# A decoder block on eight cores: the head of the first feed-forward stage is loaded, cast and ordered differently

## The reference

```python
x = x + 0.5 * swiglu_ffn(rms_norm(x, g_ffn1), w_ffn1_in, w_ffn1_out)
h = rms_norm(x, g_mix)
# retention, differential attention, memory attention on h @ w_in, gated and merged into y
x = x + y @ w_o
x = x + 0.5 * swiglu_ffn(rms_norm(x, g_ffn2), w_ffn2_in, w_ffn2_out)

def rms_norm(x, g):      # over the 1024 channels of a token
    return x * rsqrt(mean(x * x) + EPS) * g
def swiglu_ffn(h, w_in, w_out):
    gate, up = split(h @ w_in, 2)      # 2816 each
    return (silu(gate) * up) @ w_out
```

## Time and profile before

| | |
|---|---|
| median of 3 runs | 2390.73 us |
| lowest, highest | 2389.24, 2524.57 us |
| profiled execution | 2388.88 us, of which the span of its slowest core (core 2) is 2387.8 us |
| spans of the eight cores | 2382.2 to 2387.8 us |
| PE busy | 2321.8 us, 97% of the span, 13284 matmuls |
| DVE, ACT, POOL busy | 51%, 41%, 6% |
| chain that ended last | PE 90%, ACT 4%, DVE 2%, POOL 1%, DMA 1% |

### The profile page before, as it was taken

One profiled execution on the slowest core, in us unless ns is written; L12 is line 12 of the kernel. 1 busy time (PEld: TensorE's weight loads), 2 busy tenths in 40 slices (PEclk: granted clock), 3 DMA queues, 4 the chain that ended last, 5 costly groups with the idle time before them and its releaser, 6 DMA issues.

```text
span 2387.8 us, 34149 instructions; the slowest of 8 cores (2382.2 to 2387.8 us)
## 1 busy us (share of the span) xinstructions
PE 2321.8 (97%) x13284; PEld 1112.4 (47%) x13284; DVE 1222.9 (51%) x2359; ACT 984.8 (41%) x1679; POOL 149.8 (6%) x173
## 2 busy tenths in 40 slices
PE   6999999999999999999999999999999999999998
PEld 2444444444444444454444465555554444444443
DVE  5577334485565552113444576677754655344334
ACT  3111110357767764144631487788851221111110
POOL 1000000230000000000000111121100000000000
PEclk9999999999999999999999999999999999999999
DMA  8221221353442424342102200201305322321313
GB/s 232 49 50 24 52 38 34 82 135 58 67 79 37 83 43 74 54 73 51 20 16 46 46 12 10 45 13 28 48 10 141 71 45 36 53 36 24 47 18 141
DMA packets 86779, 132.69 MB, mean 56 GB/s; under 512 B 71648, under 2 KB 72032, under 8 KB 75360
## 3 DMA queue, kind: packets, MB, share of 16 engines
q0 software_dynamic: 10512, 75.50, 18.8%
q1 hardware_dynamic: 76112, 55.00, 9.1%
HBM read 172.43 MB, written 16.78 MB: 79 GB/s over the span
## 4 chain that ended last, share of the span: by engine, by line
PE 90%; ACT 4%; DVE 2%; POOL 1%; DMA 1%; issue 1%; SPq 0%; POOLq 0%; DVEq 0%; ACTq 0%
PE pw L605 90%; ACT ET L616 2%; POOL acc L628 1%; ACT nrs L616 1%; DMA stg<-w_ffn_in 1%; DMA memT<-mem 0%; ACT L616 0%; DVE dq L620 0%; DVE dU L639 0%; ACT sqf L616 0%; SPq L647 0%; DVE mqn L620 0%; DVE dn L620 0%; ACT nsq L616 0%; ACT sgt L616 0%
## 5 line engine op out<-in xcount | busy, mean ns | idle before, releaser
L605 PE MATMUL pw<-hT,wbuf 128*128 128x512 bf16 x4864 | 1168.5, 381 | 12.3 <-ACT nrs L616 5.6
L605 PEld LDWEIGHTS pw<-hT,wbuf 128*128 128x128 bf16 x4864 | 471.5, 98 | 551.9 <-issue 29.4
L616 ACT ACTIVATE sgf<-pw 128x512 f32<-128x512 f32 x176 | 104.1, 596 | 702.6 <-PE pw L605 702.5
L605 PE MATMUL pw<-uu,wbuf 128*128 128x512 bf16 x1408 | 334.1, 379 | 0.0
L605 PE MATMUL pw<-wbuf,hT 128*128 128x512 bf16 x1280 | 303.2, 379 | 0.2 <-DVE sgR L628 0.2
L616 ACT ACTIVATE ET<-pw 128x1024 bf16<-128x1024 f32 (+1 forms) x288 | 265.9, 975 | 66.9 <-PE pw L605 64.0
L628 DVE TENSOR_TENSOR uu<-pw,sgf 128x512 bf16<-128x512 f32 x176 | 120.8, 690 | 275.7 <-PE pw L605 275.5
L605 PEld LDWEIGHTS pw<-uu,wbuf 128*128 128x128 bf16 x1408 | 137.7, 98 | 166.1 <-issue 0.2
L605 PEld LDWEIGHTS pw<-wbuf,hT 128*128 128x128 bf16 x1280 | 123.0, 98 | 137.5 <-issue 0.6
L605 PE MATMUL pw<-Vd,ET 128*128 128x129 bf16 x2176 | 173.2, 220 | 8.3 <-DVE dU L639 4.5
L620 DVE SCALAR_TENSOR_TENSOR xT<-pw,xT 128x512 f32<-128x512 f32 x192 | 130.4, 688 | 78.4 <-PE pw L605 74.7
(11 more groups left out here) (120 smaller groups left out, 2153.6 us busy)
## 6 DMA issues: line engine op xcount, KB each, us to landing
wbuf<-w_in POOLq DMA_DIRECT2D x26, 1024.0 KB, 8.3
wbuf<-w_ffn_in POOLq DMA_DIRECT2D x21, 1024.0 KB, 10.3
wbuf<-w_ffn_out POOLq DMA_DIRECT2D x10, 1024.0 KB, 9.6
xs<-xT SPq DMA_DIRECT2D x4, 2048.0 KB, 11.6
xT<-x SPq DMA_DIRECT2D x6, 1024.0 KB, 22.9
wbuf<-w_br_ret POOLq DMA_DIRECT2D x4, 1024.0 KB, 8.0
wbuf<-w_mem_kv POOLq DMA_DIRECT2D x4, 1024.0 KB, 10.5
x2l<-xs SPq DMA_DIRECT2D x2, 2048.0 KB, 14.5
```

The source lines that it names most:

```text
L605: return Op("pe", lambda e: e.matmul(out, lhsT=lhsT, rhs=rhs, start=start, stop=stop, **kw), reads, writes, n / 2400.0 + 0.003, 0.17, sign ...
L616: return Op("act", lambda e: e.activation(out=out, in_=in_, func=func, **kw), reads, writes, c, 0.08, fuse=("accum_out" not in kw), tab=TA ...
```

## The change

Five edits, all in the head of the stage:

- Tile 0 of `x` comes in two transfers of 1 MB and not four of 0.5 MB, `cbf` between the two and `pvec` behind them. The first half of tiles 2 and 3 is now issued only when the tile before has landed.
- The eight casts of the first block move from POOL to ScalarE, behind the first tile's Exp.
- The first three weight transfers on POOL wait for the first half of tile 1, the second half of tile 2 and the first half of tile 3.
- The order of the products becomes: block 0 with tiles 0 and 1, block 1 with tiles 0 and 1, then blocks 0 and 1 with tile 2, then with tile 3. Block 0 with tiles 2 and 3 is worked bank by bank, no output products are woven into the first four of these, and the evacuation of tile 0 is held back until the Exp of tile 1 has been emitted.
- A matrix of ones is written into `uu19`, and products of it with itself, whose results nobody reads, go into a free bank: 9 ahead of the first tile's squares, 12 between its fourth and fifth, 9 behind its eighth (`warm`).

The diff, cut to its core:

```diff
+        def warm(n):
+            for _ in range(n):
+                yield Op("pe", lambda e: e.matmul(bk(6), lhsT=uu[19][:, 0:128], rhs=uu[19][:, :], start=True, stop=True),
+                         [uub[19]], [bkb[6]], 0.22, 0.17)
...
+                if done == ("f1", "h", 0):
+                    yield Op("dve", lambda e: e.memset(uu[19][:, :], 1.0), [], [uub[19]], 0.2)
+                    yield from warm(9)
...
+                    if done == ("f1", "h", 0) and k in (3, 7):
+                        yield from warm(12 if k == 3 else 9)
...
+                if key[0:4] == ("f1", "u", 0, 0):
+                    yield flag(("f1", "h", 1, 0))
...
-            for b in range(11):
+            order = [(b, t) for b in range(11) for t in range(NT)]
+            if tag == "f1":
+                order[0:8] = [(0, 0), (0, 1), (1, 0), (1, 1), (0, 2), (1, 2), (0, 3), (1, 3)]
+            for n_, (b, t) in enumerate(order):
+                outs = 2 if tag == "f2" or n_ >= 4 else 0
...
-                parts = 4 if t == 0 else 2
+                for i in range(2):
+                    sl = slice(i * 2048, i * 2048 + 2048)
+                    dep = [x1b(t - 1, 7)] if t >= 2 and i == 0 else []
...
         def w_cast():
+            yield flag(("f1", "h", 0, 0))
...
-                yield Op("pool", lambda e, dst=dst, src=src: e.tensor_copy(out=dst, in_=src), [stgb[k]], [w0b[k]], 0.6)
+                yield act(dst, src, AF.Copy, [stgb[k]], [w0b[k]], TT)
...
-            yield flag(("f1", "x0"))
-            for dep in (x1b(3, 0), x1b(3, 0), x1b(3, 7)):
-                yield W.load([dep])
+            for t, k in ((1, 0), (2, 7), (3, 0)):
+                yield flag(("f1", "x", t))
+                yield W.load([x1b(t, k)])
```

More of the change, by code:

```diff
@@ L810, in ffn @@
                 wbk = w0b if (tag, b) == ("f1", 0) else [wb] * KC
[L811 to L833, removed]
+                us, keys = held.setdefault(((b + 1) // 2, t), ([], []))
+                if b == 0 and (tag == "f2" or t < 2):
+                    bks = []
                     for j in range(2):
@@ L837, in ffn @@
                         keys.append((tag, "u", b, t, j))
-                        bks = []
                         for half in range(2):
[L840 to L853, removed]
+                            yield f_all.free
+                            bks.append(f_all.get())
+                    for k in range(KC):
+                        yield flag((tag, "h", t, k))
+                        if tag == "f1":
+                            yield flag(("w0", k))
+                        for i in range(4):
+                            c = k * 512 + (i % 2) * 256 + (i // 2) * 128
+                            yield mm(bk(bks[i]), wt[:, c:c + 128], hs(t, k), k == 0, k == KC - 1, [wbk[k], hTb[t][k]],
+                                     [bkb[bks[i]]], TT)
@@ new lines, in ffn @@
+                    for j in range(2):
+                        sch.spawn(evac(bks[2 * j], bks[2 * j + 1], us[j], keys[j]), 0)
+                    pend.append(outp(0, t, us, keys))
+                    if t == NT - 1:
+                        W.give((tag, "a", b))
+                    continue
+                for j in range(2):
+                    yield uu_s.free
+                    us.append(uu_s.get())
+                    keys.append((tag, "u", b, t, j))
+                    bks = []
+                    for half in range(2):
+                        yield f_in.free
+                        p = f_in.get()
+                        bks.append(p)
+                        for k in range(KC):
+                            yield flag((tag, "h", t, k))
+                            c = k * 512 + half * 256 + j * 128
+                            yield mm(bk(p), wt[:, c:c + 128], hs(t, k), k == 0, k == KC - 1, [wbk[k], hTb[t][k]],
+                                     [bkb[p]], TT)
+                        if half == 0:
+                            yield from steps(outs)
+                    sch.spawn(evac(bks[0], bks[1], us[-1], keys[-1]), 0)
+                    yield from steps(outs)
@@ L854, in ffn @@
+                if b % 2 == 0:
+                    pend.append(outp(b // 2, t, us, keys))
+                if t == NT - 1:
+                    W.give((tag, "a", b))
             yield from steps(99)
@@ L874, in load_consts @@
             for t in range(NT):
-                parts = 4 if t == 0 else 2
-                n = KC // parts
-                for i in range(parts):
-                    if t == 0 and i == 1:
+                for i in range(2):
+                    sl = slice(i * 2048, i * 2048 + 2048)
+                    dep = [x1b(t - 1, 7)] if t >= 2 and i == 0 else []
+                    yield spdma(xT[:, t * 4096 + i * 2048:t * 4096 + (i + 1) * 2048], x_d[t][:, sl], dep,
+                                [x1b(t, k) for k in range(i * 4, i * 4 + 4)], 1 << 20)
+                    if t == 0 and i == 0:
                         yield spdma(cbf[:, :], cbf_d[:, :], [], [b_cbf], 200000)
[L880 to L883, removed]
+                if t == 0:
+                    yield spdma(pvec[:, :], pvec_d[:, :], [], [b_const], 32768)
                 sch.spawn(norm(lambda k, t=t: x1(t, k), lambda k, t=t: x1b(t, k), t, PV_GFFN1, ("f1", "h", t)), 3)
@@ L889, in load_consts @@
                     sch.spawn(w_cast(), 2)
-            flags.add(("f1", "x0"))
+                flags.add(("f1", "x", t))
             yield spdma(keep[:, :], keep_d[:, :], [], [b_keep], 98304)
```

## The result

The changed kernel takes 2375.95 us as a median of 5 runs, against 2390.55 of the kernel before on the same chip. The ratio is 0.994, 95% interval 0.9922 to 0.9957: some 14.5 us less. I had forecast 2383.0 with a range from 2377.5 to 2388.0. The sign and the place were right.

A forecast was written before the change was run, and what follows sets the result against it. TensorE was taken as full behind the head, so only the head's gaps could be won. Gains of 0.95 and 5.9 sum to 6.9 us: 2388.9 to 2382.0; the median stands 1.8 higher, so forecast 2383.0, range 2377.5 to 2388.0.

The forecast's parts named there:

- step 2: Tile 1 in the head: lands at 26.5 us, main run starts at 32.3 instead of 33.25, gain 0.95 us.
- step 3: From tile 1's main run to the first output product: 3.3 us lost in place of 9.2, gain 5.9 us.
- All engines run the same order afterwards: Behind the head: a change of the head can win only what the head loses.
- Step 1: Tile 0 in the head: first product at 19.4 us against 17.21, covered because tile 1 cannot start before its second half lands.
- my slow case: Tile 0: the twelve products of ones run at 0.43 us until 15.4 us, costing 2.2 us at its first product.
- The clock dip: Tile 1's main run: after a quiet stretch 3.0 us run at half pace, losing 1.6 us.
- The stall of 1.2 us: Block 1 to tile 2: tile 2's eighth `hT` ready after 9.8 us, TensorE needs it after 8.6.
- The block that holds back tile 1: Rival: early weight block delays tile 1's landing to 28.4 or 31.4 us, gain 5.0 or 2.0; chance 0.17.
- Ones that never lift the clock: Rival: tile 0 begins at 0.43 us a product, tile 1's run starts at 33.6 to 34, 2383.6 us; chance 0.12.
- It goes better: Rival: tile 1 unhindered, no dip on tile 1, no stall; gain 11.5 us, 2377.4; chance 0.12.
- Tile 2 late: Rival: tile 2 lands at 47.5 and 50.6 us, 7.8 lost against 6.9 gained, 2389.8; chance 0.07, shared with block late.
- marks for "right": Head: tile 0's first product 17 to 20 us, tile 1's run 31 to 33.5, no DMA waits, first output near 59.

The follow-up runs named there:

- second profiles: The kernel before and the changed kernel, both unchanged, each profiled again; 2389.85 us (ratio 0.9997) and 2376.76 us (0.9942).
- run 31: Not a follow-up run: in "From Ln to the run 31.20 - 27.79", tile 1's main run of products in the changed kernel, starting at 31.20 us.
- late: Changed kernel with the first three weight transfers tied to the landing of tile 3 again, as before the change; 2391.19 us, ratio 1.0005.
- nochain: Changed kernel with all of x issued at once, tiles 2 and 3 no longer waiting for the tile before to land; 2387.05 us, ratio 0.9987.
- nohold: Changed kernel without the wait that holds back tile 0's evacuation until tile 1's Exp; 2378.34 us, ratio 0.9949.
- nowarm: Changed kernel without the thirty products of ones; 2380.46 us, ratio 0.9958.
- no_first9: Changed kernel without the first nine products of ones; 2376.22 us, ratio 0.994.

## Why the prediction was wrong, step by step

The gain at the last product was 13.8 us, and my sum had 6.9. Of the some 7 us missing, 2.2 lie in step 2, 1.5 in step 3, and 3.3 behind the head, which I had at nothing. Without the 2.3 us gained near 930 us the time would have been some 2378.3, inside the range.

**What bounds the kernel: right in the main, wrong in one clause, and here the mechanism failed.** "All engines run the same order afterwards" is true, and I took it to mean that nothing moves behind the head. The same order does not give the same time when something outside it, the loading of the program, moves against it. The cost was the 2.3 us gained near 930 us (1.9 between the second profiles), and it was not a term mis-sized but one that I put at nothing without a row to show it.

**Step 1, tile 0: right.** Most of its working came out within 1.3 us: the eighth sum ended at 16.1 (forecast 17.2), the first product of tile 0 came at 18.57 (19.4). `hT` began 1.7 us earlier than forecast (17.57 against 19.3), for it follows the Exp at once. The twelve ones took 4.85 us on this core (5.1) and ran at half pace until 14.09. On the others the pace rose anywhere from 9.2 to 14.5 us, so my slow case was that of the slowest core and not the common one. A cast took 4.25/8 = 0.53 us (0.54), a piece of `hT` 0.67 (0.67). The first half of tile 0 landed at 6.7 and not 8.0; as I said, none of this was on the path.

**Step 2, tile 1: mis-sized, 0.95 forecast, 3.1 measured.** From Ln to the run 31.20 - 27.79 = 3.4 us, exactly the chain I had added up. Three terms were off. The landing: I took 26.5, half shared with the block. It was 24.8 as a mean of the eight cores (24.5 over the six of the ledger), and `late`, without the early block, gives 24.8 too. The block is issued 2 us before tile 1 has landed, and delayed nothing. From the landing to Ln I took 2.4 us, and it took 3.0 over these six; before it had taken 4.2 over all eight, so this stretch too became shorter, which I had not worked out. Together they are 1.4 of the miss (32.3 forecast, 30.94 measured). The rest, 0.8, is the row I measured from: 33.25 is one core's value, and the mean of six was 34.05 (33.58 in the second profile).

**Step 3, what follows: right in kind, too cautious.** Lost from 31.20 to 56.59: 25.39 less 110 products at 0.2157, 1.7 us, where I had 3.3. The clock dip came as forecast: the loads run at half pace from 31.46 to 34.56, 3.1 us (3.0), which costs 1.5 (1.6); this is the slowest core, and on three of the six there was no dip. The stall of 1.2 us before tile 2's eighth `hT` did not come. I had let the chain of ScalarE start when a whole group of block 1 was done; Silu needs the gate's eight products alone, so it starts 8 x 0.2157 = 1.7 us earlier. Small waits took 0.2 (0.5). By the means the gain of the stretch was 7.4, against 5.9.

**What I had not seen at all** is that step 3's whole gain hangs on the chain, and step 2's on the hold-back. I gave neither a price. They are worth 11 us (`nochain` against the changed kernel) and 2.4 (`nohold`) of the time, because they decide what the scheduler emits.

**The rivals.** The block that holds back tile 1: refuted by `late`. Ones that never lift the clock: refuted, tile 0's first 20 products run at 0.2157 us each on all six cores. "It goes better", 2377.4 at 0.12, had two of its three terms right (tile 1 unhindered, no stall) and the third, no dip, on half of the cores. It was still 1.5 us short, for the passage. Tile 2 late: it did not decide, but it was nearer than I had it. Its halves landed at 36.9 and 39.7 us as means, the second beyond my 32 to 38; on the slowest core it came at 39.5, and its first square starts at 42.15. The margin is 2.6 us there. On core 0, where the second half came at 41.5, a square waited 1.3 us for it, and TensorE did not.

**The marks.** The first output product was forecast near 59 and came at 56.59; block 1 followed tile 1 directly; TensorE waited for no transfer in between. All marks for "right" were met, or surpassed, and the range missed all the same: they were marks of the head alone.

**Open.** The other 1.0 us of the first pair of profiles (3.0 in the second pair) is made of a loss of 0.6 between the 232nd product and the passage (a gain of 0.9 in the second pair) and a gain of 1.6 (2.1) behind it, in many shifts of 0.1 to 1.0 us. I have not traced it. Nor do the runs say how much of it is scatter between profiles.

## What to carry to other kernels

When a change alters how many instructions an engine has, look once at where the instruction queue's packets fall against the loads on the path: here 30 products of nothing moved the last product by 5.3 us in one kernel and by 2.0 in the other, through a place 900 us later. In a kernel whose order comes from a scheduler's model, a dependency is also a statement to the model: cost it by the order that is emitted with it and without it. And take the starting row of a difference from the mean over cores, not from the slowest one: one core's value was 0.8 us off the mean (0.3 off that of the second profile).

## What the runs showed of the hardware

- Issuing the load of `mem` on SP took 0.56 us, or 1.9 to 2.5 when a packet of the instruction queue fell on it (`nowarm`, all cores), and the 1 MB load landed 8.45 us after its issue instead of 5.3 to 5.9. Where the packet came 0.7 to 1.7 us behind the issue (five cores of the kernel before), the issue took 0.56 us and the load still 5.9 to 8.0.
- 2 MB of weights issued 2 us before a tile's second half had landed delayed that half by nothing and the next tile's second half by 6.4 us (39.7 in the changed kernel against 33.3 in `late`).
- TensorE's weight loads ran 0.43 us apart, the level of 1.2 GHz, from 2.0 us on while the granted clock showed 1.00. In the changed kernel they closed up to 0.22 us at 9.2 to 14.5 us, by core, 12.2 as a mean of eight (12.0 in the second profile); without the first nine products (`no_first9`) at 11.3 to 15.2, 12.8 as a mean. The cores scatter by more than the nine products change.
